# One head of the delta rule a product unit later, and rotary tables that carry the norm weights

## The reference

```python
h = rms_norm(x, attn_norm_w)
proj = h @ w_in
# group A: gated delta rule, chunked (short convolution, SiLU, l2-normed q and k)
o_a = gated_delta_rule_chunked(dq, dk, dv, g, beta)
o_a = rms_norm(o_a, delta_out_norm_w) * silu(z)
# group B: dilated window attention
aq = rope(rms_norm(aq, q_norm_w), positions)
ak = rope(rms_norm(ak, k_norm_w), positions)
o_b = rms_norm(dilated_mixture_attention(aq, ak, av), attn_out_norm_w)
x = x + concat(o_a, o_b) @ w_out
x = x + (silu(gate) * up) @ w_down      # gate, up = split(rms_norm(x) @ w_gate_up)
```

## Time and profile before

| | us |
|---|---|
| median of three executions | 2704.82 |
| lowest, highest | 2704.6, 2706.18 |
| span of the profiled execution, first to last instruction | 2701.7 |
| PE busy in the span | 2574.5 |
| DVE busy | 1125.6 |
| ACT busy | 828.9 |
| POOL busy | 255.3 |

### The profile page before, as it was taken

One profiled execution on the slowest core, in us unless ns is written; L12 is line 12 of the kernel. 1 busy time (PEld: TensorE's weight loads), 2 busy tenths in 40 slices (PEclk: granted clock), 3 DMA queues, 4 the chain that ended last, 5 costly groups with the idle time before them and its releaser, 6 DMA issues.

```text
span 2701.7 us, 36699 instructions
## 1 busy us (share of the span) xinstructions
PE 2574.5 (95%) x12602; PEld 2188.6 (81%) x12602; DVE 1125.6 (42%) x1769; ACT 828.9 (31%) x1497; POOL 255.3 (9%) x235
## 2 busy tenths in 40 slices
PE   4999999999999988898999999999999999999999
PEld 2888979888898877786888888888888888888887
DVE  3546465565646564223333333333333333333333
ACT  3322232323223231224433223432233432222221
POOL 0122223212122320002000000000000000000000
PEclk9999999999999998999999999999999999999999
DMA  3322222222222221432333333333333333333334
GB/s 106 89 65 60 67 56 60 63 66 61 58 66 57 61 66 36 146 96 58 98 97 97 97 94 95 97 97 97 94 91 99 97 97 96 90 99 97 96 97 128
DMA packets 346196, 228.73 MB, mean 85 GB/s; under 512 B 16930, under 2 KB 312228, under 8 KB 344996
## 3 DMA queue, kind: packets, MB, share of 16 engines
q1 hardware_dynamic: 342080, 222.35, 29.8%
q10 hardware_dynamic: 4068, 5.75, 0.6%
HBM read 223.85 MB, written 4.19 MB: 84 GB/s over the span
## 4 chain that ended last, share of the span: by engine, by line
PE 63%; DVE 2%; POOL 1%; DMA 1%; issue 0%; ACT 0%; ACTq 0%; POOLq 0%; DVEq 0%
PE bank L485 61%; PE bank L446 1%; POOL h2c L1373 1%; DMA big<-in_x 1%; DVE big L1270 0%; PE bank L442 0%; DVE wlo L373 0%; ACT gs L938 0%; DVE y L1156 0%; DVE in_lo L1210 0%; PE bank L593 0%; PE bank L603 0%; ACT whi L368 0%; PE bank L602 0%; DVE Q L1092 0%
## 5 line engine op out<-in xcount | busy, mean ns | idle before, releaser
L373 DVE TENSOR_TENSOR wlo<-raw,whi 128x512 fp32r<-128x512 f32 (+1 forms) x848 | 597.6, 709 | 1082.1 <-ACT whi L368 1069.9
L368 ACT ACTIVATE whi<-raw 128x512 fp32r<-128x512 f32 (+1 forms) x848 | 514.8, 613 | 1198.2 <-PE bank L485 1197.7
L485 PE MATMUL bank<-in_hi,whi 128*128 128x512 f32 x1920 | 768.2, 400 | 5.9 <-DVE big L1270 3.8
L485 PE MATMUL bank<-in_hi,wlo 128*128 128x512 f32 x1920 | 751.1, 391 | 0.0
L485 PE MATMUL bank<-in_lo,whi 128*128 128x512 f32 x1920 | 751.0, 391 | 0.0
L485 PEld LDWEIGHTS bank<-in_hi,whi 128*128 128x128 f32 x1920 | 363.1, 189 | 82.4 <-issue 9.3
L485 PEld LDWEIGHTS bank<-in_hi,wlo 128*128 128x128 f32 x1920 | 362.3, 189 | 77.6
L485 PEld LDWEIGHTS bank<-in_lo,whi 128*128 128x128 f32 x1920 | 363.2, 189 | 75.1 <-issue 1.9
L485 PE MATMUL bank<-whi,in_hi 128*128 128x384 f32 (+1 forms) x768 | 285.7, 372 | 11.6 <-DVE wlo L373 9.4
L485 PE MATMUL bank<-wlo,act_hi 128*128 128x512 f32 x704 | 277.4, 394 | 0.0
L485 PE MATMUL bank<-whi,in_lo 128*128 128x384 f32 (+1 forms) x768 | 276.6, 360 | 0.0
(11 more groups left out here) (224 smaller groups left out, 1823.6 us busy)
## 6 DMA issues: line engine op xcount, KB each, us to landing
raw<-in_w_gate_up SPq DMA_DIRECT2D x352, 256.0 KB, 2.9
raw<-in_w_down SPq DMA_DIRECT2D x176, 256.0 KB, 3.1
raw<-in_w_in SPq DMA_DIRECT2D x128, 256.0 KB, 2.8
raw<-in_w_in SPq DMA_DIRECT2D x128, 192.0 KB, 2.7
raw<-in_w_out SPq DMA_DIRECT2D x64, 256.0 KB, 3.1
big<-in_x SPq DMA_DIRECT2D x4, 1024.0 KB, 10.9
big<-in_x ACTq DMA_DIRECT2D x4, 1024.0 KB, 10.1
out<-big SPq DMA_DIRECT2D x16, 256.0 KB, 3.8
```

The source lines that it names most:

```text
L368: e.activation(whi[c % RING][:, 0:n], raw[c % RING][:, 0:n], ACT.Copy).then_inc(hi_made, 1)
L373: e.tensor_tensor(wlo[c % RING][:, 0:n], raw[c % RING][:, 0:n], whi[c % RING][:, 0:n], ALU.subtract).then_inc(lo_made, 1)
L485: o = pe.matmul(dst_, a, b, start=(start and n == 0), stop=(stop and n == 2))
```

## The change

Three edits. In the two tables, the delta steps from `d_khat` on come one unit later (`d_tokens` stays), the steps of the attention stay where they are, and `d_turn` now stands ahead of `a_out` in stage D15. The rotary tables are multiplied once, at the start, with the norm weights of q and k into a new tile `rope`, so that `a_krot` has five passes and q's rotation four, and q's norm factor goes into the scale of the softmax, so that q isn't multiplied by it at all. POOL makes the two table products of q before it waits for the sum of squares.

```diff
-A_STAGES = {1: ["cum", "d_tokens", "a_sq"], 3: ["d_khat"], 4: ["d_kk"], 5: ["a_tail"], 6: ["d_ti"], 7: ["q0"],
-            8: ["u0"], 9: ["q1"], 10: ["u1"], 11: ["q2"], 12: ["u2"], 13: ["q3"], 14: ["u3"], 15: ["q4", "a_evac"]}
-D_STAGES = {0: ["u4", "a_norm"], 1: ["q5", "a_sum"], 2: ["u5", "a_krot"], 3: ["d_wt", "conv0"],
-            4: ["v0", "a_turn", "tanh0"], 5: ["r0", "a_score0", "fin0"], 6: ["v1", "a_mask0"],
-            7: ["r1", "a_prob0", "a_score1", "conv1"], 8: ["v2", "a_pv0", "a_mask1", "tanh1"],
-            9: ["r2", "a_prob1", "a_score2", "fin1"], 10: ["v3", "a_pv1", "a_mask2"],
-            11: ["r3", "a_prob2", "a_score3", "conv2"], 12: ["d_norm", "a_pv2", "a_mask3", "tanh2"],
-            13: ["a_prob3", "fin2"], 14: ["a_pv3", "d_turn"], 15: ["a_out", "conv3"]}
+A_STAGES = {1: ["cum", "d_tokens", "a_sq"], 4: ["d_khat"], 5: ["d_kk"], 6: ["a_tail"], 7: ["d_ti"], 8: ["q0"],
+            9: ["u0"], 10: ["q1"], 11: ["u1"], 12: ["q2"], 13: ["u2"], 14: ["q3"], 15: ["u3", "a_evac"]}
+D_STAGES = {0: ["q4", "a_norm"], 1: ["u4", "a_sum"], 2: ["q5", "a_krot"], 3: ["u5", "conv0"],
+            4: ["d_wt", "a_turn", "tanh0"], 5: ["v0", "a_score0", "fin0"], 6: ["r0", "a_mask0"],
+            7: ["v1", "a_prob0", "a_score1", "conv1"], 8: ["r1", "a_pv0", "a_mask1", "tanh1"],
+            9: ["v2", "a_prob1", "a_score2", "fin1"], 10: ["r2", "a_pv1", "a_mask2"],
+            11: ["v3", "a_prob2", "a_score3", "conv2"], 12: ["r3", "a_pv2", "a_mask3", "tanh2"],
+            13: ["d_norm", "a_prob3", "fin2"], 14: ["a_pv3"], 15: ["d_turn", "a_out", "conv3"]}
...
+        rope = mb("rope", [P, 2, 2, TT_N, P])
...
@@ ACT, a_score
-                    act.activation(ex[:, 0:n], sm[:, 0:n], ACT.Exp, scale=SCALE,
+                    act.activation(ex[:, 0:n], sm[:, 0:n], ACT.Exp, scale=a_rn()[:, t, 0:1],
@@ DVE, start
-            dve.tensor_scalar(wqk[:, :, :], wqk[:, :, :], root, None, ALU.mult).then_inc(cols_made, 1)
+            dve.tensor_scalar(wqk[:, 0], wqk[:, 0], root * SCALE, None, ALU.mult).then_inc(cols_made, 1)
+            dve.tensor_scalar(wqk[:, 1], wqk[:, 1], root, None, ALU.mult).then_inc(cols_made, 1)
@@ DVE, after the splits of the first three units
+            dve.wait_ge(act0, 2)
+            dve.wait_ge(cols_made, 7)
+            for c in range(2):
+                for n in range(2):
+                    trig = cs[:, n].unsqueeze(2).broadcast_to([P, TT_N, 2, P // 2])
+                    gain = wqk[:, c].rearrange("p (a n) -> p a n", a=2).unsqueeze(1).broadcast_to([P, TT_N, 2, P // 2])
+                    dve.tensor_tensor(halves(rope[:, c, n]), trig, gain, ALU.mult).then_inc(rope_made, 1)
@@ DVE, a_krot
-                    dve.wait_ge(pool_a, 12 * h + 3)
-                    rotate(lambda i, o: step(o, krot, 6 * h + i), dve, 1, qkv[:, :, P:2 * P], a_rn()[:, :, 1:2], 1,
-                           aT[:, 0:SEQ], aT[:, SEQ:])
+                    dve.wait_ge(pool_a, 10 * h + 5)
+                    step(dve.tensor_tensor(X, X, a_rn()[:, :, 1:2].broadcast_to([P, TT_N, P]), ALU.mult), krot, 5 * h + 1)
+                    step(dve.tensor_tensor(four(a_), X, rope[:, 1, 0], ALU.mult), krot, 5 * h + 2)
+                    step(dve.tensor_tensor(four(b_), X, rope[:, 1, 1], ALU.mult), krot, 5 * h + 3)
+                    step(dve.tensor_tensor(X4[:, :, 0], a4[:, :, 0], b4[:, :, 1], ALU.subtract), krot, 5 * h + 4)
+                    step(dve.tensor_tensor(X4[:, :, 1], a4[:, :, 1], b4[:, :, 0], ALU.add), krot, 5 * h + 5)
@@ DVE, a_score
-                    dve.tensor_scalar(ast[:, 28 + t:29 + t], ast[:, 24 + t:25 + t], -SCALE, None,
-                                      ALU.mult).then_inc(sm_ready, 1)
+                    dve.tensor_scalar(ast[:, 28 + t:29 + t], ast[:, 24 + t:25 + t], a_rn()[:, t, 0:1], -1.0,
+                                      ALU.mult, ALU.mult).then_inc(sm_ready, 1)
@@ POOL, a_norm
+                    astep(h, 2, pool.tensor_tensor(four(ra[:, :]), X, rope[:, 0, 0], ALU.mult))
+                    astep(h, 3, pool.tensor_tensor(four(rb[:, :]), X, rope[:, 0, 1], ALU.mult))
                     pool.wait_ge(a_ss, h + 1)
-                    rsqrt(lambda i, o: astep(h, i, o), 2, ast[:, 16:24], ast[:, 8:16], ast[:, 0:8], 4)
-                    rotate(lambda i, o: astep(h, i, o), pool, 4, qkv[:, :, 0:P], a_rn()[:, :, 0:1], 0, ra[:, :], rb[:, :])
+                    rsqrt(lambda i, o: astep(h, i, o), 4, ast[:, 16:24], ast[:, 8:16], ast[:, 0:8], 4)
+                    astep(h, 6, pool.tensor_tensor(X4[:, :, 0], a4[:, :, 0], b4[:, :, 1], ALU.subtract))
+                    astep(h, 7, pool.tensor_tensor(X4[:, :, 1], a4[:, :, 1], b4[:, :, 0], ALU.add))
```

More of the change, by code:

```diff
@@ L220, in a_rn, with halves @@
             return ast[:, 16:24].rearrange("p (t c) -> p t c", c=2)
[L222 to L234, removed]
+        def halves(t):
+            return t.rearrange("p t (a n) -> p t a n", a=2)
         ident = const(C_ID)
@@ L302, in hybrid_layer @@
         pool_a = sem("pool_a")
+        rope_made = sem("rope_made")
         krot = sem("krot")
@@ L613, in a_tail @@
                 def a_tail():
-                    pe.wait_ge(pool_a, 12 * d + 12)
+                    pe.wait_ge(pool_a, 10 * d + 10)
                     pe.wait_ge(qss, d + 1)
@@ L619, in a_turn @@
                     for c, b in ((0, 2), (1, 3)):
-                        pe.wait_ge((pool_a, krot)[c], (12 * h + 9, 6 * h + 6)[c])
+                        pe.wait_ge((pool_a, krot)[c], (10 * h + 7, 5 * h + 5)[c])
                         pe.wait_ge(qkv_ready, 4 * h + 3 + c)
@@ L872, in a_turn @@
                 def a_turn():
-                    act.wait_ge(krot, 6 * h + 6)
+                    act.wait_ge(krot, 5 * h + 5)
                     for c in range(2):
@@ L1135, in a_sum @@
                 def a_sum():
-                    dve.wait_ge(pool_a, 12 * h + 1)
+                    dve.wait_ge(pool_a, 10 * h + 1)
                     dve.reduce_sum(ast[:, 0:8], aT[:, :].rearrange("p (g n) -> p g n", g=8), AXX).then_inc(a_ss, 1)
                 def a_krot():
-                    dve.wait_ge(pool_a, 12 * h + 3)
-                    rotate(lambda i, o: step(o, krot, 6 * h + i), dve, 1, qkv[:, :, P:2 * P], a_rn()[:, :, 1:2], 1,
-                           aT[:, 0:SEQ], aT[:, SEQ:])
+                    X, a_, b_ = qkv[:, :, P:2 * P], aT[:, 0:SEQ], aT[:, SEQ:]
+                    X4, a4, b4 = halves(X), halves(four(a_)), halves(four(b_))
+                    dve.wait_ge(pool_a, 10 * h + 5)
+                    if first:
+                        dve.wait_ge(rope_made, 4)
+                    step(dve.tensor_tensor(X, X, a_rn()[:, :, 1:2].broadcast_to([P, TT_N, P]), ALU.mult), krot, 5 * h + 1)
[3 more added lines that the diff above has]
+                    step(dve.tensor_tensor(X4[:, :, 1], a4[:, :, 1], b4[:, :, 0], ALU.add), krot, 5 * h + 5)
                 def conv(c):
@@ L1306, in astep @@
                 def astep(head, i, ins):
-                    step(ins, pool_a, 12 * head + i)
+                    step(ins, pool_a, 10 * head + i)
                 def rsqrt(one, i, out_, tmp, in_, first_eps):
@@ L1342, in a_sq @@
                     pool.wait_ge(oass, 4 * d + 4)
-                    rsqrt(lambda i, o: astep(d, i, o), 10, ast[:, 8:12], ast[:, 4:8], ast[:, 0:4], 4)
-                    astep(d, 12, pool.tensor_tensor(four(oa[:, :]), four(oa[:, :]), per_tile(ast[:, 8:12]), ALU.mult))
+                    rsqrt(lambda i, o: astep(d, i, o), 8, ast[:, 8:12], ast[:, 4:8], ast[:, 0:4], 4)
+                    astep(d, 10, pool.tensor_tensor(four(oa[:, :]), four(oa[:, :]), per_tile(ast[:, 8:12]), ALU.mult))
                 def a_norm():
@@ L1350, in a_norm @@
                     astep(h, 1, pool.tensor_tensor(four(aT[:, :]), qkv[:, :, 0:2 * P], qkv[:, :, 0:2 * P], ALU.mult))
+                    X = qkv[:, :, 0:P]
+                    X4, a4, b4 = halves(X), halves(four(ra[:, :])), halves(four(rb[:, :]))
+                    if first:
+                        pool.wait_ge(rope_made, 4)
+                    astep(h, 2, pool.tensor_tensor(four(ra[:, :]), X, rope[:, 0, 0], ALU.mult))
+                    astep(h, 3, pool.tensor_tensor(four(rb[:, :]), X, rope[:, 0, 1], ALU.mult))
                     pool.wait_ge(a_ss, h + 1)
-                    rsqrt(lambda i, o: astep(h, i, o), 2, ast[:, 16:24], ast[:, 8:16], ast[:, 0:8], 4)
-                    rotate(lambda i, o: astep(h, i, o), pool, 4, qkv[:, :, 0:P], a_rn()[:, :, 0:1], 0, ra[:, :], rb[:, :])
+                    rsqrt(lambda i, o: astep(h, i, o), 4, ast[:, 16:24], ast[:, 8:16], ast[:, 0:8], 4)
+                    astep(h, 6, pool.tensor_tensor(X4[:, :, 0], a4[:, :, 0], b4[:, :, 1], ALU.subtract))
+                    astep(h, 7, pool.tensor_tensor(X4[:, :, 1], a4[:, :, 1], b4[:, :, 0], ALU.add))
                 return dict(d_tokens=d_tokens, d_kk=d_kk, d_norm=d_norm, a_sq=a_sq, a_norm=a_norm)
```

## The result

The changed kernel took 2660.1 us (median of four, 2657.1 to 2662.9) against 2705.5 us (four runs, 2704.6 to 2706.3): a ratio of 0.9836, 95% interval 0.9822 to 0.985.

The account below looks back on a forecast made before the run. PE, busy 95% of the span, bounds the kernel, with its waits and low clock: -7.8 - 19.9 - 2.0 - 3.5 - 1.9 + 2.7 + 1.3 + 0.15 = -31 us, so 2673.8 against 2704.8 us; range 2662 to 2688.

Parts of the forecast that it names:

- The wait for the rotated q: PE's wait for POOL before `a_turn` goes in 8 bodies: 19.9 us, plus 2.0 us for falls of the clock.
- rival 1: DVE's rotation stays long, so PE waits before `d_wt`; 2681 to 2689 us, at 2685; chance 0.17.
- The wait for kh: PE's wait before `kh`'s turns mostly stays, 1.85 us left; gain 0.6 us in each of 7 bodies, 4.2 us.
- What I gave for the clock: Behind `kh`, two of four falls of the clock go, at 0.57 + 0.5 us each: 2.1 us (0 to 4.3).
- the 1.5 us for the small waits: Waits before `a_tail` and `d_ti` shrink by 0.5 us in three bodies without a fall of the clock.
- a_prob3: PE's wait for the mask of `a_prob3`, 0.5 us a body, all goes: 3.5 us.
- The new wait in A0: `d_turn` ahead of `a_out` delays the division; PE waits at tile 3, 0.45 us in six bodies: 2.7 us added.
- The exit: End of the last body: the output projection starts later behind `d_turn`, `a_out` and z; 1.3 us added (0 to 2).
- The four table products at the start: Products for `rope`, 2.8 to 5.7 us, hidden inside the 11.54 us in which DVE waits for PE: nothing added.
- Rival 2: The `kh` wait falls to its lower price and all low-clock stretches of the heads vanish; 2666 us; chance 0.12.
- Rivals 3 and 4: 3: waits only passed on, half the gain lost, 2690, chance 0.11; 4: k's rotation delays `d_wt`, 2715, chance 0.05.
- My own sign of being wrong: Body-to-body distance falling by less than 3 or more than 5.5 us, or an unlisted wait summing to over 3.

Follow-up runs that it names:

- turn_late: The changed kernel with `d_turn` behind `a_out` in stage D15; 2657.5 us, ratio 0.9837 to the kernel before.
- three power steps: The changed kernel with three small power instructions (8 columns) added on POOL ahead of q's two half passes; 2669.4 us, ratio 0.9873 to the kernel before.
- four steps: The changed kernel with four small power instructions (8 columns) added on POOL ahead of q's two half passes; 2701.4 us, ratio 0.999 to the kernel before.
- norm_late: The kernel before with only `d_norm` moved one stage later, to D13; ratio 0.9994 to the kernel before.

## Why the prediction was wrong

**The wait for the rotated q** is the step that failed. Its mechanism held: POOL is done early and DVE's rotation takes 3.9 us. In body 6 after, DVE and POOL from the inverse norm on, and PE's `d_wt` and turns:

```profile
785.15 1.64 POOL L1319 TENSOR_TENSOR ast<-ast,mhalf 128x8 f32<-128x8 f32 x1
...
786.83 0.69 DVE L1144 TENSOR_TENSOR qkv<-qkv,ast 128x512 f32<-128x512 f32 x1
...
786.88 1.24 POOL L1365 TENSOR_TENSOR qkv<-ra,rb 128x256 f32<-128x256 f32 x1
...
787.56 1.10 DVE L1145 TENSOR_TENSOR aT<-qkv,rope 128x512 f32<-128x512 f32 x1
...
788.19 1.06 POOL L1366 TENSOR_TENSOR qkv<-ra,rb 128x256 f32<-128x256 f32 x1
...
790.29 0.42 DVE L1148 TENSOR_TENSOR qkv<-aT 128x256 f32<-128x256 f32 x1
...
790.84 0.69 DVE L364 TENSOR_TENSOR wlo<-raw,whi 128x512 fp32r<-128x512 f32 x1
...
791.45 0.68 DVE L1096 TENSOR_TENSOR TI<-TI,bank 128x512 f32<-128x512 f32 x1
...
792.26 1.15 PE L437 MATMUL bank<-TI,kbg 128*128 128x128 f32 x8
...
793.25 1.04 PE L433 MATMUL bank<-K,qkv 128*128 128x128 f32 x8
```

The inverse norm is ready at 786.79; DVE ends the fifth pass at 790.71, 3.9 us later, and the subtraction of `u5` at 792.13, 0.13 us before `d_wt` starts (I had 0.3 to spare). POOL ends at 789.25, 4.0 us before the turns at 793.25, with 1.24 and 1.06 us for the half passes that I had at 0.78. So rival 1 fell, by little, and with some luck: the passes that I listed for DVE add up to 3.63 us and an end at 819.85, not the 820.1 that I went on with; the five passes took 3.73 us (both table passes 1.10, where I had 1.42 and 0.69) and 0.15 more between them. What I mis-sized is the term. I priced the stop at its recorded 2.5 us, added 0.7 us of clock in three bodies, and `vn` in the three bodies whose trace names it: 19.9 + 2.0 + 1.9. But every one of bodies 1 to 7 paid either 0.8 us for `vn` or 1.6 us of low clock, within which DVE caught up, so that the wait for `vn` wasn't recorded. DVE's copy of `vn` before, in body 3, whose turns start at 467.24:

```profile
471.41 0.28 DVE L1104 COPY vn<-bank 128x128 f32<-128x128 f32 x1
```

It ends 4.45 us after the turns start, as it does in body 2 and in all of bodies 1 to 7. With the full clock PE comes earlier and waits, and its product starts at 4.50; with the low clock PE comes at 5.30, when `vn` has long been ready. The 0.7 us between a body with full and one with low clock is the difference of the two, not the price of the clock. The clock had also fallen at the turns of bodies 0 and 6, not only of 3, 4 and 5. And the stop itself cost 0.2 us more than its record. Measured: 3.5 us in bodies 1, 2 and 7, 4.3 in 3 to 6, 4.1 in body 0, together 32.0 for 23.8. This alone is 8.2 of the missing 9.6 us. The other terms were off by -2.5, +1.5, -1.3 and +0.3 us, -2.0 together, and the last row of the table adds 3.5, which is chance as far as the runs show.

**The wait for kh** was right to 0.1 us (1.91 in the mean for 1.85). Body 7, splits and masks, as in the earlier trace rows:

```profile
845.35 3.85 DVE L364 TENSOR_TENSOR wlo<-raw,whi 128x384 fp32r<-128x384 f32 x3 [2.88 <-ACT whi L359]
...
847.31 1.46 POOL L1329 TENSOR_TENSOR QK<-QK,K 128x512 f32<-128x512 f32 x1
...
849.11 0.68 DVE L1079 TENSOR_TENSOR kh<-bank,dst 128x512 f32<-128x512 f32 x1
...
849.85 0.66 PE L433 MATMUL bank<-K,kh 128*128 128x128 f32 x4 [1.84 <-DVE kh L1079]
```

Three passes take 3.85 us beside POOL, `kh` starts 0.34 us after line 1329 ends, and PE waits 1.84. My working had small slips that change little: 763.14 + 0.4 is 763.54, not 763.45, and PE comes at 762.31, not 762.35. What I gave for the clock was too much: it still falls in three of seven bodies (a segment of 19.4 us, against 18.7), one less than before and not two, and T is waited for as before where it doesn't, so the 1.5 us for the small waits didn't come. 5.3 us for 7.8.

**a_prob3**: all of it goes, and it is 0.72 us a body, not the 0.5 recorded, because the unit before it carried 0.15 us of the loss and the turns 0.05. **The new wait in A0** costs 0.67 us a body for 0.45. Its chain, as in the earlier trace rows, and PE's tile 3:

```profile
833.71 0.60 PE L433 MATMUL bank<-K,Q 128*128 128x128 f32 x4
...
834.47 0.75 DVE L1122 SCALAR_TENSOR_TENSOR big<-bank,wdo_half,zs 128x512 f32 x1 [2.55 <-PE bank L433]
...
835.46 0.69 DVE L1193 TENSOR_TENSOR pT<-bank,ast 128x512 f32<-128x512 f32 x1
```

```profile
835.57 0.34 PE L476 MATMUL bank<-whi,in_lo 128*128 128x384 f32 x1
836.21 0.44 PE L476 MATMUL bank<-whi,in_hi 128*128 128x384 f32 x1 [0.30 <-DVE pT L1193]
836.49 0.33 PE L476 MATMUL bank<-wlo,in_hi 128*128 128x384 f32 x1
```

From the turns to the end of the division it is 2.44 us, as worked out (2.45), and PE takes tile 3 at 2.50. The record shows only 0.31 us of stop before it, because it counts from the end of the matmul at 835.57, and ends overlap the next start: in the same unit matmuls otherwise start every 0.18 us, here after 0.64, so tile 3 comes 0.46 us late. The next one follows after 0.28, another 0.10. The last 0.1 us is not the wait's: unit A0 takes 2.20 us without it in `turn_late`, against 2.11 before, because turns now stand right ahead of it. **The exit** cost 1.0 us for 1.3 (1.4 by my own terms: 4.0 - 2.2 - 0.4). The four table products at the start took 2.49 us together, ahead of a wait of 10.27 us for PE, so they were hidden.

**The 3.6 us behind the start of the output projection** were no part of the change. PE's window of 82 us from the start of the output projection, which holds the epilogue: before,

```profile
988.00:1070.00 82.00, 68.73 (x358) 0.84 0.13 36
```

after,

```profile
951.00:1033.00 82.00, 68.63 (x367) 0.90 0.12 36
```

and in the run with three power steps, whose code is the same from here on:

```profile
960.80:1042.80 82.00, 68.60 (x396) 0.98 0.16 42
```

The same code is granted 0.84 of the clock, 0.90 and 0.98, and gets through 358, 367 and 396 instructions. From the start of the output projection to the end of the span it is 1713.7 us before, 1710.1 after, 1703.6 with three power steps, and it has lain between in the others with this code (1711.3, 1708.5, 1705.1, 1711.2, 1710.2, 1708.3, 1711.4). The changed kernel itself, run again, has 1706.6, 3.5 us less than the first time. What varies is the epilogue, its first 14 units: 93.5 us before, 89.8 after, 86.6 after again, 83.6 with three power steps, while the FFN takes 1450.6 to 1452.0 in all. So one execution of this kernel can't settle a difference of 5 us, on either side of the comparison, and my statement that 0.2% can be told from no change was too confident. The two comparisons of the changed kernel give 45.4 and 41.1 us (2702.3 - 2661.1 for the second), ratios 0.9836 and 0.9853. Both lie clear of the 31 forecast.

Rival 2 (2666) is nearer to the time than the forecast, but not by its mechanism: the wait for `kh` stayed at its upper price. Rivals 3 and 4 did not come. My own sign of being wrong would have missed this: from body to body it is 113.8 us for 118.65 where the clock stays up, 4.85 less, inside the 3 to 5.5 that I allowed, because seven bodies with 0.7 us more each than the forecast 4.1 make 5 us of the miss.

## What to carry to other kernels

Price a stop on the bound engine by the distance between its instructions across the whole stretch, in a body with the stop and against what the same instructions take without it, and not by the recorded wait: what comes late behind it, and a low clock that hides that, goes or stays with it. When two engines work in parallel towards one step, cost the removal of each alone first; the one that hides behind the other is the next stop, and it can be longer than it shows now (here 3.0 us for 0.8). And when a step moves a stage later in a hand-written order, follow what the other engines' queues put ahead of it: a later place in PE's order is no help as long as DVE does one more split first.

## What the runs showed of the hardware

After stops of 1.0 to 1.2 us at `a_turn` PE's clock stayed at 2.4 GHz in seven of seven bodies (three power steps); after 3.1 to 3.4 us it was at 1.2 GHz for part of the next four in six of seven (four steps); after 2.5 us it went both ways with the same code (bodies 1 and 2 against 3 to 6 before). After the 1.9 us before `kh` it fell in three of seven bodies, in both profiles; after the 2.4 us before the change in four, and in all seven in `norm_late`, with the same code at that place. A fall costs some 1.6 us, in each of the two places where it was measured: 1.67 between the turns and the product, and 1.58 in unit A5, where body 3 of the changed kernel fell in one profile and not in the other; there the small waits behind it shrink by 0.9. And a wait costs PE 0.05 to 0.3 us more than its record: 1.21 for 1.16 at `a_turn`, 2.79 for 2.59 there in body 0, 0.57 for 0.31 in A0.
